# The loop over sixteen head pairs of a hybrid decoder layer, written out on all five engines

## What is computed

```python
xn = _rmsnorm(x, norm_mix)
P = xn @ w_in                        # columns for both branches and the merge gates
z = prw + mu_shift * (prw_prev - prw)
uc, new_cbuf = _causal_conv(u, cbuf, conv_w, conv_b)
h, h_last = _rg_lru(uc, h0, first, rg_wa, rg_ba, rg_wx, rg_bx, rg_lam)
br_a = (h * gelu(gate)) @ w_rg_o
o_b, S_last = _rwkv7(z, S0, ...)     # per head: S = S*w + (S @ -kk) b^T + v k^T ; y = S @ r
br_b = o_b @ w_rw_o
x = x + (sigmoid(Pa) * br_a + sigmoid(Pb) * br_b) @ w_o
hf = relu(_rmsnorm(x, norm_ffn) @ w_up); x = x + (hf * hf) @ w_down
x = x + sigmoid(_rmsnorm(x, norm_ple) @ w_ple_gate) * (p @ w_ple)
y = _rmsnorm(x, norm_f)
```

## Time and profile before

| | us |
|---|---|
| median of 3 runs | 3011.85 |
| lowest, highest run | 3005.26, 3018.11 |
| span of the profiled execution | 2998.1 |
| steps 1 to 15 in that span | 124.12 to 1531.04 |

### The profile page before, as it was taken

How to read it: one execution, slowest core, us unless ns; L and a number is a source line. 1 busy time by engine, 2 the same in 40 slices (tenths; PEclk the granted TensorE clock), 3 DMA queues, 4 the chain that set the end, 5 groups by cost and what they waited for, 6 DMA issues and landing times.

```text
span 2998.1 us, 57750 instructions
## 1 busy us (share of the span) xinstructions
PE 2774.0 (93%) x22780; PEld 2572.5 (86%) x22780; DVE 1676.5 (56%) x2866; ACT 1197.0 (40%) x1680; POOL 125.8 (4%) x105
## 2 busy tenths in 40 slices
PE   6999988998889988899889999989999999999897
PEld 5887877787777877778778999989999999999897
DVE  5766665566655665566653445564444444444664
ACT  3544344334443444344443333334442433433243
POOL 0100111011110111001100000000000000000000
PEclk8999889898898999898999999999999999999998
DMA  5433232333233223332334676645565565566543
GB/s 161 128 99 86 63 83 71 85 82 78 71 84 86 70 77 84 84 86 69 77 86 118 185 217 179 175 137 154 168 168 158 164 168 156 166 168 165 164 126 103
DMA packets 699775, 363.50 MB, mean 121 GB/s; under 512 B 43905, under 2 KB 698531, under 8 KB 698659
## 3 DMA queue, kind: packets, MB, share of 16 engines
q1 hardware_dynamic: 699598, 360.74, 44.4%
HBM read 346.12 MB, written 14.59 MB: 120 GB/s over the span
## 4 chain that ended last, share of the span: by engine, by line
PE 82%; DVE 7%; issue 6%; ACT 2%; DMA 2%; SPq 0%; DVEq 0%; ACTq 0%
PE bank L612 81%; PE bank L640 2%; DVE wl L1634 1%; DVE nrm L1314 1%; DVE sd L1311 1%; DVE inv L1311 1%; ACT L1062 1%; DVE zk L1314 1%; DMA raw<-w_in 1%; DVE xl L1311 1%; DVE both L1311 0%; DVE wl L1308 0%; DVE yc L1314 0%; DVE sums L1336 0%; DMA nsq<-gb_scratch 0%
## 5 line engine op out<-in xcount | busy, mean ns | idle before, releaser
L612 PE MATMUL bank<-xh,wh 128*128 128x288 f32 (+1 forms) x3136 | 1032.1, 329 | 94.2 <-issue 56.0
L612 PE MATMUL bank<-xl,wh 128*128 128x288 f32 (+1 forms) x3136 | 956.5, 305 | 22.2 <-issue 22.2
L612 PE MATMUL bank<-xh,wl 128*128 128x288 f32 (+1 forms) x3136 | 953.3, 304 | 0.0
L612 PEld LDWEIGHTS bank<-xh,wh 128*128 128x128 f32 x3136 | 613.9, 196 | 142.0 <-issue 93.5
L612 PEld LDWEIGHTS bank<-xl,wh 128*128 128x128 f32 x3136 | 616.2, 196 | 34.9 <-issue 26.9
L612 PEld LDWEIGHTS bank<-xh,wl 128*128 128x128 f32 x3136 | 615.5, 196 | 0.0
L1308 DVE TENSOR_TENSOR wl<-raw,wh 128x2048 fp32r<-128x2048 f32 x206 | 472.1, 2292 | 214.4 <-ACT wh L1006 214.4
L1006 ACT ACTIVATE wh<-raw 128x2048 fp32r<-128x2048 f32 x206 | 393.2, 1909 | 428.8 <-PE bank L612 411.3
L612 PE MATMUL bank<-sbl,wh 128*128 128x288 f32 x1792 | 534.6, 298 | 0.0
L612 PE MATMUL bank<-sbh,wl 128*128 128x288 f32 x1792 | 533.0, 297 | 0.0
L612 PE MATMUL bank<-sbh,wh 128*128 128x288 f32 x1792 | 529.7, 296 | 1.8 <-DVE wl L1308 1.8
(11 more groups left out here) (283 smaller groups left out, 2896.0 us busy)
## 6 DMA issues: line engine op xcount, KB each, us to landing
raw<-w_in SPq DMA_DIRECT2D x116, 1024.0 KB, 5.8
raw<-w_up SPq DMA_DIRECT2D x64, 1024.0 KB, 6.3
raw<-w_down SPq DMA_DIRECT2D x64, 1024.0 KB, 5.9
raw<-w_rg_o SPq DMA_DIRECT2D x16, 1024.0 KB, 6.0
raw<-w_rw_o SPq DMA_DIRECT2D x16, 1024.0 KB, 6.0
raw<-w_o SPq DMA_DIRECT2D x16, 1024.0 KB, 5.9
raw<-w_ple_gate SPq DMA_DIRECT2D x16, 1024.0 KB, 6.0
s<-state_rwkv SPq DMA_DIRECT2D x32, 128.0 KB, 3.7
```

The lines of the kernel that those rows point to most:

```text
L612: return pe.matmul(out, lhsT, rhs, start=start, stop=stop, skip_group_check=True)
```

## The change

On each engine the loop over the steps becomes a loop of the program that writes the kernel, so that all steps are written out one behind the other, with constants where registers were. `isinstance(it, int)` is now true in every step: `apart` adds nothing, and conditions such as `later` or `it == 0` are settled when the kernel is written. Addresses and the sources and targets of SP's transfers become constants as well. The order of the instructions, the slots, the tables and all buffers are the same, and nothing behind the main loop changes.

```diff
--- before.py
+++ after.py
@@ -472,10 +472,8 @@
             small_early(0)
             for u in range(3):
                 load_unit(in_columns(unit_columns(u, 0)), u % 2, U_LOOP + u)
-            step(0, False, False)
-            with sp.Fori(1, KT - 1) as it:
-                step(it, False, True)
-            step(KT - 1, True, True)
+            for it in range(KT):
+                step(it, it == KT - 1, it > 0)
 
             for u in range(LOOP_UNITS):
                 load_unit(in_columns(OFF_GB + (u + 3) * P), (u + 3) % 2, U_GB + u + 3)
@@ -909,10 +907,8 @@
                         for name in EARLY.get(slot, []):
                             early(name, it)
 
-            step(0, "loop", False)
-            step(1, "loop", True)
-            with pe.Fori(2, KT) as it:
-                step(it, "loop", True)
+            for it in range(KT):
+                step(it, "loop", it > 0)
             step(KT, "gb", True)
 
             def phase(base, hi, lo, first, last, read, before=None, extra=None, start=2, ready=None):
@@ -1197,10 +1193,8 @@
                         for name in EARLY.get(slot, []):
                             early(name, it)
 
-            step(0, "loop", False)
-            step(1, "loop", True)
-            with act.Fori(2, KT) as it:
-                step(it, "loop", True)
+            for it in range(KT):
+                step(it, "loop", it > 0)
             step(KT, "gb", True)
             gb_evict(5)
             hi(U_GB + 7, 1, (U_GB + 7) // 2)
@@ -1674,10 +1668,8 @@
                 if chain:
                     ch.end()
 
-            step(0, "loop", False)
-            step(1, "loop", True)
-            with dve.Fori(2, KT) as it:
-                step(it, "loop", True)
+            for it in range(KT):
+                step(it, "loop", it > 0)
             step(KT, "gb", True)
             lo(U_GB + 7, 1)
 
@@ -1820,9 +1812,7 @@
                                              sbk[:, h * HEAD:(h + 1) * HEAD].unsqueeze(1).to_broadcast([2 * SAMP, NB, HEAD]), own, ALU.mult)
                 ins.then_inc(sexp_ready, 1)
 
-            masked(0)
-            samples(0)
-            with pool.Fori(1, KT) as p:
+            for p in range(KT):
                 masked(p)
                 samples(p)
```

## The result

| | before | after |
|---|---|---|
| median of the runs, us | 3008.56 (4 runs) | 2886.8 (4 runs) |
| span of the profiled execution, us | 2998.1 | 2875.7 |
| steps 1 to 15 in it, us | 1406.9 | 1288.2 |
| PE's gaps named "issue", us | 78.2 in 26 | none |
| packets of instructions | 160 | 122 |

The account below looks back on a forecast made before the run. PE, busy for 93% of the span, bounds the kernel. Steps 1 to 15 fall from 1406.9 to 1285.5 us, gain 121.4, less 5 for clock, plus 0.5 for registers; 3011.85 - 117 = 2895 us, range 2870 to 2917.

Parts of the forecast that it names:

- The place and size: PE's 13 loop jumps: 78.2 us of gaps go; with low clock in units 0 and 5, 9.25 us a jump, 120 us.
- The pace of step 2: Steps 2 to 15 written out: fourteen go at step 2's 85.71 us, step 1 stays at 85.57; gain 121.4 us.
- second half-clock stretch: Unit 3: one in four of fourteen steps takes 18.61 instead of 17.18 us; 5 us taken off the gain.
- (a): Rival: clock falls badly in every step, unit 1 at 21.05 and unit 3 at 18.61; 2928 us, chance 0.09.
- (b): Rival: unit 1 keeps its short form of 18.16 us without the gaps; 84.1 us a step, 2868 us, chance 0.04.
- The 13.75 us: Whole run: the runs' median of 3011.85 us lies 13.75 above the profiled span of 2998.1; kept in the forecast.
- Registers: Waits, addresses and DMA sources in the steps become constants: between nothing and 2 us in all, 0.5 us taken.
- The others' jumps: DVE, ACT, POOL and SP loops: hidden, on no chain PE waits for before the pairwise products; otherwise 3 us gain.
- The rest of the program: Step 0, gate units and everything from 1531.04 on keep their code; shifted half-clock stretches move them 2 or 3 us either way.
- The cause of the gaps: PE's jump leaves the code at hand: target fetched (4.35 us gap), then the next block (2.15 us).
- (c): Rival: straight code on PE is fetched too late, 2.15 us a block, seven a step; 3102 us, chance 0.03.
- DVE as the tightest cover: Unit 0 of step 2: DVE is busy for 10.56 of 11.31 us, and PE's gaps no longer give it time.

Follow-up runs that it names:

- experiment 1: Kernel before with PE's loop alone written out, the other engines keeping loops and registers: 2887.23 us, ratio 0.9609; two further kernels put PE's loop back or halved its jumps.
- shifted kernel: Kernel before, all loops and registers kept, with 32 always-fulfilled waits ahead of PE's loop, moving its body by 16 places: 2892.12 us, ratio 0.9627.

## Why the prediction was right, and where it was not

The forecast was 2895 us, the measured median 2886.8; in gain, 117 against 122. The place, the size and the pace were right; the condition behind the gaps and the chain behind DVE's jump were not.

- *The place and size.* PE's 26 gaps and the low clock behind them, 120 us by the two units on either side of a jump, are what went; experiment 1 showed that PE's loop alone carries it. Unit 0 was to be 11.3, unit 5 12.7 and unit 1 19.7 us, and they are 11.32, 12.7 and 19.7 (18.1 in four steps).
- *The pace of step 2.* The sum had 85.57 + 14 x 85.71 us, less 5 us of gain for one step in four with a second half-clock stretch: 1290.5 us. Measured 1288.2. Three steps in fifteen were longer by 1.5 us; the second stretch came in seven steps (granted clock 0.94, and 0.96 in the other eight), and in four of these unit 1 was shorter by as much, which I had not foreseen. That the pace agrees to 0.2 us a step is in part luck: it is that of the fastest of four executions. Rivals (a) and (b) both took one unit's extreme for a step's; in this profile the short unit 1 always comes with the long unit 3. Steps as bad as (a) had them do occur at this pace in other kernels: two of 90.5 us in the shifted one, with unit 3 at 19.2 and unit 4 at 13.5 us (clock 0.78 and 0.81 there), and one in the kernel with PE alone written out.
- *The 13.75 us* between span and median were no fixed part of a run: in the changed kernel span and run differ by 1.8 us. The other 12 us were the distance of one execution from the median, and keeping them was right for a forecast of the median.
- *Registers*, 0.5 us taken: nothing to be seen. The shifted kernel keeps them, and units 2 to 5 of its step 3 take the times of the changed kernel within 0.03 us. *The others' jumps* were costed at nothing, as "on no chain that PE waits for before the pairwise products". This step failed: DVE's is on a chain that ends earlier, at the `bonus` product of unit 0 (and the pairwise products stand in the same unit, not two units later). It would cost 5 us where PE is written out and DVE is not. The bound of 14 x 0.2 = 3 us was too small, as it took the first gap of 0.22 us alone and a jump costs 0.38. The sum was not hurt, for it went by the pace of step 2, into which DVE does not jump either.
- *The rest of the program*, 2 or 3 us either way: 3.5 us less in step 16.
- *The cause of the gaps.* "The jump leaving the stretch of code at hand" was the right kind of cause, with the wrong condition. I set the 2048 instructions of the Trainium skill against the gaps and wrote that the trace disagrees. It does not: the body of 1604 fits, but as theory C has it only where it covers seven blocks, and in the kernel before it stood so that it covered eight. 16 places of shift remove 116 us. I also left out a sentence of the same section (Runtime: NRT & Kernel Launch, Instruction fetch mechanics), by which a taken branch forces a fetch when its target is not in the current window of two pages. It would have spoken for the gaps; but the shifted kernel disagrees with it, for its jump goes back over more than six blocks with no packet and no gap. That the Trainium skill's 108 ns for a branch (Advanced Engine Details and Errata, Control Flow Timing) were far off at PE came from the same thing; of a jump within code that is held PE's trace shows no idle time, and DVE's 0.38 us, in which register instructions are included, is larger than that figure.
- *Rival (c)*, straight code fetched too late: seventeen steps of it, with no gap and 122 packets in all. I had expected 7 to 8 a step; step 5 has 6, and the 1562 instructions that it issues on PE are 6.1 blocks of 256.
- *DVE as the tightest cover*: PE's waits for the weights' split in the steps come to 2.0 us, as before. What grew without the gaps is the wait for the sigmoid, 31.7 us in place of 23.4.

## What to carry to other kernels

Where a loop's steps are longer than the same code entered by falling through, look at the engine's gaps named "issue" behind the jump and at the packets of the instruction queue in one step: none means that the body is held, one for every 256 instructions or so means that it is fetched at every turn. If the body is just short enough to be held, as here with 1603 instructions, its place in its blocks may be worth nearly as much as writing it out (116 of 122 us here); a few instructions ahead of the loop settle it in one run. Price a change of this kind by a stretch of the same trace that already runs the new way (here step 2), not by adding up what stands in the gaps, for the clock behind a gap counts too (9.3 us a jump against 6.0 us of gaps). And before a loop's jump is called hidden, look at every product that PE takes from that engine behind it, not only at the largest group.

## What the runs showed of the hardware that was not expected

- A PE loop body of 1603 issued instructions costs no fetch and no time at its jump in two placements (shifted by 16 and by 80 instructions: 43 packets, looped steps of 83 to 90.6 us), and is fetched anew every time in two others (unshifted and shifted by 231: 160 and 161 packets). The placements fit a store of eight 16 KB blocks of which a loop can use seven; the number of blocks was not measured apart from these four points and the figure of the Trainium skill.
- The first gap at such a jump costs PE 4.3 us on average in the kernel before (3.9 to 4.6) and 4.4 in the one shifted by 231. A second one of 1.3 to 2.2 us follows in the kernel before, ten instructions behind the target at each of the 13 jumps, and none where the target was moved by 231. That a block ends there, and that the fetch is covered where it ends some 36 instructions behind the target, is my reading of these two placements.
- Two waits on the same semaphore leave as one instruction, of some 0.1 us (462 waits in 231 instructions, 23.9 us).
